# Seven block products of the second feed-forward matrix in digit passes, with some of the low digits made on GpSimd

## The reference, cut to what matters

```python
# first block, for each of its two layers
h = rmsnorm(x, norm_mlp[i])
x = x + jnp.square(jax.nn.relu(h @ w_ff1[i])) @ w_ff2[i]     # 1024 -> 4096 -> 1024
...
# second block, for each of its two layers
def sq_relu_mlp(x, w1, w2):
    return jnp.square(jax.nn.relu(x @ w1)) @ w2
```

## Time and profile before

| | |
|---|---|
| time, median of 3 runs | 1448.4 us (1447.07 to 1448.81) |
| span of the profiled execution, first to last instruction | 1445.8 us |
| TensorE matmul busy | 1414.5 us, 98% of the span |
| VectorE busy | 1092.6 us, 76% |
| ScalarE busy | 815.7 us, 56% |
| GpSimd busy | 289.4 us, 20% |
| mean granted TensorE clock | 0.998 of full |

### The profile page before, as it was taken

The page is one execution under the profiler, slowest core; times in us unless marked ns, Lnnn a source line. Parts: engine busy times, 40 slices in busy tenths (PEclk is TensorE's granted clock), DMA queues, the critical chain, the costliest instruction groups (busy, mean ns, idle before and its releaser), DMA issues.

```text
span 1445.8 us, 20133 instructions
## 1 busy us (share of the span) xinstructions
PE 1414.5 (98%) x8416; PEld 1188.4 (82%) x8416; DVE 1092.6 (76%) x1326; ACT 815.7 (56%) x998; POOL 289.4 (20%) x109
## 2 busy tenths in 40 slices
PE   7999999999999999999999999999999999999997
PEld 5788888888877788888889788688888888888886
DVE  5337667989952365859999769878998857689988
ACT  4565636666445553646657356656666326277662
POOL 4598150000028695410000000000000005000000
PEclk9999999999999999999999999999999999999999
DMA  8833336555546642445756443305565453155551
GB/s 306 302 122 122 139 128 222 204 202 193 189 144 236 214 148 91 156 168 199 234 179 200 167 162 110 137 28 206 204 219 189 151 203 117 46 207 210 207 194 68
DMA packets 121227, 250.28 MB, mean 173 GB/s; under 512 B 15041, under 2 KB 27057, under 8 KB 121009
## 3 DMA queue, kind: packets, MB, share of 16 engines
q1 hardware_dynamic: 120872, 248.90, 48.9%
q10 hardware_dynamic: 264, 0.10, 0.0%
HBM read 247.94 MB, written 1.05 MB: 172 GB/s over the span
## 4 chain that ended last, share of the span: by engine, by line
PE 80%; DVE 11%; ACT 5%; issue 1%; POOL 1%; DMA 1%; DVEq 0%; ACTq 0%
PE psum L522 77%; PE psum L529 4%; DVE w_lo L1283 2%; POOL w_lo L1283 1%; DVE w_lo L1290 1%; DVE w_lo L1393 1%; DVE big L1381 1%; DVE x L1462 1%; ACT w_hi_big L1319 1%; DMA ring<-in_mlp_w 1%; DVE ring L1381 1%; ACT s_hi L1327 1%; DVE big L2962 1%; ACT w_hi_tmp L1253 1%; ACT w_hi_tmp L1263 0%
## 5 line engine op out<-in xcount | busy, mean ns | idle before, releaser
L522 PE MATMUL psum<-ht_hi,w_lo 128*128 128x256 f32 x960 | 279.7, 292 | 5.5 <-ACT work L1337 4.1
L522 PE MATMUL psum<-w_lo,ht_hi 128*128 128x512 f32 (+1 forms) x576 | 222.2, 389 | 0.8 <-DVE w_lo L1283 0.8
L522 PEld LDWEIGHTS psum<-ht_hi,w_lo 128*128 128x128 f32 x960 | 180.0, 187 | 15.5 <-issue 14.4
L522 PEld LDWEIGHTS psum<-w_lo,ht_hi 128*128 128x128 f32 x576 | 108.4, 188 | 22.1 <-DVE w_lo L1283 1.3
L522 PE MATMUL psum<-ht_lo,w_hi_tmp 128*128 128x256 f32 x448 | 125.1, 279 | 0.0
L522 PE MATMUL psum<-ht_lo,w_hi_rows 128*128 128x256 f32 x448 | 125.0, 279 | 0.0
L522 PE MATMUL psum<-ht_hi,w_hi_tmp 128*128 128x256 f32 x448 | 124.8, 279 | 0.0
L522 PE MATMUL psum<-ht_hi,w_hi_rows 128*128 128x256 f32 x448 | 124.8, 279 | 0.0
L1283 POOL TENSOR_TENSOR w_lo<-ring,w_hi_work 128x2048 fp32r<-128x2048 f32 x12 | 57.5, 4789 | 250.3 <-ACT w_hi_work L1263 250.3
L1310 ACT ACTIVATE w_hi_work<-ring 128x2048 fp32r<-128x2048 f32 x28 | 53.6, 1915 | 74.1 <-DMA ring<-in_w_ff 39.1
L522 PEld LDWEIGHTS psum<-ht_lo,w_hi_tmp 128*128 128x128 f32 x448 | 85.2, 190 | 5.8 <-issue 5.7
(11 more groups left out here) (443 smaller groups left out, 3935.4 us busy)
## 6 DMA issues: line engine op xcount, KB each, us to landing
ring<-in_w_ff SPq DMA_DIRECT2D x32, 2048.0 KB, 8.0
ring<-in_mlp_w SPq DMA_DIRECT2D x32, 2048.0 KB, 8.4
ring<-in_w_in SPq DMA_DIRECT2D x19, 2048.0 KB, 7.8
ring<-in_w_out SPq DMA_DIRECT2D x4, 2048.0 KB, 7.7
ring<-in_w_ple_gate SPq DMA_DIRECT2D x4, 2048.0 KB, 7.8
ring<-in_sb_ssm_w_in SPq DMA_DIRECT2D x4, 2048.0 KB, 8.1
ring<-in_dsa_w_in SPq DMA_DIRECT2D x3, 2048.0 KB, 8.0
ring<-in_w_up_nsa SPq DMA_DIRECT2D x2, 2048.0 KB, 8.1
```

Of the source, the lines that this page charges most:

```text
L522: ins = pe.matmul(o, lhsT, rhs, start=start, stop=stop)
```

## The change

- Product seven runs in digits: its two float32 matmuls become six digit passes. For that ScalarE also copies the third weight sum (`t_hi[2]`, last in `act_right_forms`), GpSimd subtracts it (`t_lows[2]`, in the new `pool_mlp_seven`), and VectorE makes the low digits of the second hidden blocks (`dve_hidden_second`, last in the round).
- The low digits of the second half of the columns of ff1.2 to ff1.7 are made by GpSimd in place of VectorE, with a signal of their own (`w_lo_cols`).
- TensorE waits for the two new signals, `second_low` and `last_sum_low`, ahead of bank 6.
- `pool_tail` waits for the first product of the last ff2 tile (`ff2_ready`) in place of the last `form_used`.

```diff
--- before.py
+++ after.py
@@ -147,8 +147,10 @@
 SPLITS = [f"in{c}" for c in range(N_IN)] + ["up_nsa", "up_ret"] + ["out0", "out1"]
 LAST = 7
 SEVEN = ("", "A.", "B.")
-DIGIT_SUMS = 2
-DIGIT_FORMS = 2 + DIGIT_SUMS
+DIGIT_SUMS = 3
+HIGH_FORMS = 2 + DIGIT_SUMS
+LOW_FORMS = HIGH_FORMS - 1
+HIDDEN_FORMS = 4
 
 
 def _seven_tiles(pre):
...
@@ -469,12 +471,15 @@
-    w_lo_ready = sig("w_lo_ready", 2 * (len(SPLITS) - pool_share))
+    column_share = sum(_by_columns(name) for name in SPLITS)
+    w_lo_ready = sig("w_lo_ready", 2 * (len(SPLITS) - pool_share) - column_share)
+    w_lo_cols = sig("w_lo_cols", column_share)
-    t_summed, form_hi, form_lo = sig("t_summed", 4 * LAST), sig("form_hi", DIGIT_FORMS * LAST), sig("form_lo", DIGIT_FORMS * LAST)
+    t_summed, form_hi, form_lo = sig("t_summed", 4 * LAST), sig("form_hi", HIGH_FORMS * LAST), sig("form_lo", LOW_FORMS * LAST)
+    last_sum_low, second_low = sig("last_sum_low", LAST), sig("second_low", LAST)
@@ -607,8 +612,8 @@
                            line.ready if u == 1 and k == KT - 1 else None)
 
         def wait_split(name, half):
-            signal, n = lower_digits(name, splits)
-            pe.wait_ge(signal.sem, st.at(signal, 2 * n + half + 1))
+            signal, n = lower_digits(name, half, splits)
+            pe.wait_ge(signal.sem, st.at(signal, n))
 
         def next_columns(name):
...
@@ -793,22 +798,19 @@
                                  stop and u == 1, signal if u == 1 else None)
 
                 pe.wait_ge(s_low.sem, st.at(s_low, m + 1))
-                pe.wait_ge(form_lo.sem, st.at(form_lo, DIGIT_FORMS * m + 2))
+                pe.wait_ge(form_lo.sem, st.at(form_lo, LOW_FORMS * m + 2))
                 by_digits(bank[5], 2, right_hi[:, :, 1, :], w[:, :, 1, BANK:D], False, None)
                 by_digits(bank[7], 0, right_hi[:, :, 0, :], w[:, :, 0, BANK:D], final, form_used)
-                pe.wait_ge(form_lo.sem, st.at(form_lo, DIGIT_FORMS * m + 3))
+                pe.wait_ge(form_lo.sem, st.at(form_lo, LOW_FORMS * m + 3))
                 by_digits(bank[3], 1, t_hi[0], t_lows[pre][0], final, form_used)
-                if DIGIT_SUMS > 1:
-                    pe.wait_ge(form_lo.sem, st.at(form_lo, DIGIT_FORMS * m + 4))
-                    by_digits(bank[2], 3, t_hi[1], t_lows[pre][1], final, form_used)
-                else:
-                    pe.wait_ge(t_summed.sem, st.at(t_summed, 4 * m + 3))
-                    for u in range(2):
-                        mm(bank[2], s_form(sums_, 3, u), t_sums[pre][1][:, u, :], first and u == 0, final and u == 1,
-                           form_used if u == 1 else None)
-                pe.wait_ge(t_summed.sem, st.at(t_summed, 4 * m + 4))
+                pe.wait_ge(form_lo.sem, st.at(form_lo, LOW_FORMS * m + 4))
+                by_digits(bank[2], 3, t_hi[1], t_lows[pre][1], final, form_used)
+                pe.wait_ge(second_low.sem, st.at(second_low, m + 1))
+                pe.wait_ge(last_sum_low.sem, st.at(last_sum_low, m + 1))
                 for u in range(2):
-                    mm(bank[6], hid_f[:, s + 2 * u + 1, P:S], t_sums[pre][2][:, u, :], first and u == 0, False)
+                    f = s + 2 * u + 1
+                    products(bank[6], hid_hi[:, f, P:S], hid_lo[:, f, P:S], t_hi[2][:, u, :], t_lows[pre][2][:, u, :],
+                             first and u == 0, False, None)
 
             def seven_open(n):
@@ -1263,10 +1265,13 @@
             act.activation(w_hi[place][:, 0:width], ring[n % RING][:, h * width:(h + 1) * width], ACT.Copy) \
                 .then_inc(st.up(w_hi_ready), 1)
 
-    def lower_digits(name, splits):
-
-        mine = [n for n in splits if (n in POOL_SPLITS) == (name in POOL_SPLITS)]
-        return (w_lo_pool if name in POOL_SPLITS else w_lo_ready), mine.index(name)
+    def lower_digits(name, half, splits):
+
+        def signal(n, h):
+            return w_lo_pool if n in POOL_SPLITS else w_lo_cols if h and _by_columns(n) else w_lo_ready
+
+        own = signal(name, half)
+        return own, [(n, h) for n in splits for h in range(2) if signal(n, h) is own].index((name, half)) + 1
 
     def lower_split(st, eng, tiles, splits, name):
@@ -1276,21 +1281,22 @@
     def lower_half(st, eng, tiles, splits, name, h):
 
         n, nth = tiles.index(name), splits.index(name)
-        signal, _ = lower_digits(name, splits)
+        signal, _ = lower_digits(name, h, splits)
         places, width = PLACES if splits is SPLITS else PLACES2, split_halves(name)
         c = slice(h * width, (h + 1) * width)
         eng.wait_ge(w_hi_ready.sem, st.at(w_hi_ready, 2 * nth + h + 1))
         eng.tensor_tensor(w_lo[n % RING][:, c], ring[n % RING][:, c], w_hi[places[name][h]][:, 0:width].bitcast(F32), ALU.subtract) \
             .then_inc(st.up(signal), 1)
 
-    def lower_columns(st, dve, tiles, splits, name, h):
+    def lower_columns(st, eng, tiles, splits, name, h):
 
         n, nth, c = tiles.index(name), splits.index(name), slice(h * S, (h + 1) * S)
-        dve.wait_ge(w_hi_ready.sem, st.at(w_hi_ready, 2 * nth + h + 1))
-        dve.tensor_tensor(w_lo[n % RING][:, :].rearrange("p (k n) -> p k n", k=KT)[:, :, c],
+        signal, _ = lower_digits(name, h, splits)
+        eng.wait_ge(w_hi_ready.sem, st.at(w_hi_ready, 2 * nth + h + 1))
+        eng.tensor_tensor(w_lo[n % RING][:, :].rearrange("p (k n) -> p k n", k=KT)[:, :, c],
                           ring[n % RING][:, :].rearrange("p (k n) -> p k n", k=KT)[:, :, c],
                           w_hi[(PLACES if splits is SPLITS else PLACES2)[name][h]][:, :].rearrange("p (k n) -> p k n", k=KT).bitcast(F32), ALU.subtract) \
-            .then_inc(st.up(w_lo_ready), 1)
+            .then_inc(st.up(signal), 1)
 
     def form_free(st, eng, tiles, pre, n, nth):
@@ -1317,9 +1323,9 @@
         form_free(st, act, tiles, pre, n, 2)
         act.wait_ge(t_summed.sem, st.at(t_summed, 4 * m + 2))
         act.activation(right_hi, blocks(ring[at % RING][:, :])[:, :, :, BANK:D], ACT.Copy).then_inc(st.up(form_hi), 1)
-        if DIGIT_SUMS > 1:
-            act.wait_ge(t_summed.sem, st.at(t_summed, 4 * m + 3))
-            act.activation(t_hi[1], t_sums[pre][1], ACT.Copy).then_inc(st.up(form_hi), 1)
+        for i in (1, 2):
+            act.wait_ge(t_summed.sem, st.at(t_summed, 4 * m + i + 2))
+            act.activation(t_hi[i], t_sums[pre][i], ACT.Copy).then_inc(st.up(form_hi), 1)
 
     def act_hidden_forms(st, act, pre, n):
@@ -1386,10 +1392,10 @@
         at, m = tiles.index(f"{pre}ff2.{n}"), seventh(pre, n)
         w, lo = blocks(ring[at % RING][:, :]), blocks(w_lo[at % RING][:, :])
         forms = [(1, lo[:, :, :, 0:BANK], w[:, :, :, 0:BANK], col_hi), (3, lo[:, :, :, BANK:D], w[:, :, :, BANK:D], right_hi)]
-        forms += [(2 * i + 2, t_lows[pre][i], t_sums[pre][i], t_hi[i]) for i in range(DIGIT_SUMS)]
+        forms += [(2 * i + 2, t_lows[pre][i], t_sums[pre][i], t_hi[i]) for i in range(2)]
         for i in which:
             nth, low, v, hi = forms[i]
-            dve.wait_ge(form_hi.sem, st.at(form_hi, DIGIT_FORMS * m + nth))
+            dve.wait_ge(form_hi.sem, st.at(form_hi, HIGH_FORMS * m + nth))
             dve.tensor_tensor(low, v, hi.bitcast(F32), ALU.subtract).then_inc(st.up(form_lo), 1)
 
     def dve_hidden_sums(st, dve, pre, n):
@@ -1413,6 +1419,12 @@
         dve.wait_ge(hid_hi_ready.sem, st.at(hid_hi_ready, FB // 2 * mlp_nth(pre) + 2 * n + 2))
         dve.tensor_tensor(lo, h, hi.bitcast(F32), ALU.subtract).then_inc(st.up(hid_lo_ready, 2), 2)
 
+    def dve_hidden_second(st, dve, pre, n):
+
+        s = 4 * (n % 2)
+        hi, lo, h = (v[:, s:s + 4, :].rearrange("p (u v) t -> p u v t", v=2)[:, :, 1, P:S] for v in (hid_hi, hid_lo, hid_f))
+        dve.tensor_tensor(lo, h, hi.bitcast(F32), ALU.subtract).then_inc(st.up(second_low), 1)
+
     def dve_hidden_low(st, dve, pre, f):
 
         at = hid_slot(2 * f)
@@ -1433,23 +1445,29 @@
         dve_hidden_sums(st, dve, pre, 0)
         dve_hidden_first(st, dve, pre, 0)
         dve_hidden_sums_low(st, dve, pre, 0)
-        dve_form_lows(st, dve, tiles, pre, 0, range(3, DIGIT_FORMS))
+        dve_form_lows(st, dve, tiles, pre, 0, (3,))
+        dve_hidden_second(st, dve, pre, 0)
         for n in range(1, LAST):
             ahead = f"{pre}ff1.{n + 1}"
             lower_columns(st, dve, tiles, splits, ahead, 0)
-            if n == 1:
-                lower_columns(st, dve, tiles, splits, ahead, 1)
             dve_hidden_sums(st, dve, pre, n)
             dve_hidden_first(st, dve, pre, n)
-            if n > 1:
-                lower_columns(st, dve, tiles, splits, ahead, 1)
             dve_hidden_sums_low(st, dve, pre, n)
             dve_form_sums(st, dve, tiles, pre, n)
-            dve_form_lows(st, dve, tiles, pre, n, range(DIGIT_FORMS))
+            dve_form_lows(st, dve, tiles, pre, n, range(LOW_FORMS))
+            dve_hidden_second(st, dve, pre, n)
         lower_half(st, dve, tiles, splits, f"{pre}ff2.{LAST}", 0)
```

(21 more changed lines are left out.)

## The result

The changed kernel takes **1539.84 us** (median of 4 runs, 1537.46 to 1540.73), the kernel before 1447.89 beside it: a ratio of 1.0619, 95% interval 1.0585 to 1.0654 (1.0635 by these two medians alone). The prediction was 1538, range 1515 to 1562. The profiled span is 1538.1 against 1445.8: 92.3 us longer.

A forecast was written before the change was run, and what follows sets the result against it. VectorE, shut out by GpSimd, was to bound feed-forward rounds. Five rounds of +3.41 (17.05) plus entry 5.35 make 22.4 a part, 89.6 for four; added to 1445.8, plus 2.6, this gives 1538 us, range 1515 to 1562.

The forecast's parts named there:

- The exclusion: Feed-forward rounds: two-SBUF-input VectorE instructions and GpSimd's SBUF-reading ones shut each other out; 6.60 us a round; chance 0.84.
- The price of one instruction: Feed-forward rounds: VectorE loses 4.42 us to GpSimd's moved column half, 2.18 to its third-weight-sum low digits.
- The 2.36 for GpSimd's small instruction: GpSimd's low digits of the third weight sum, 1024 columns: 2.36 us, interpolated between 2.57 at 1120 and 4.61 at 2048.
- The round and the entry: Each feed-forward part: VectorE's round 24.86 against TensorE's 21.45 us, +3.41; start of the second half unit 5.35 later.
- 0 ± 1 a part: End of each feed-forward part: the last product's tail, on either engine, was put at 0 ± 1 us.
- rival 3: Feed-forward rounds: waits over 3 us lower TensorE's clock, up to 34 us on top of the exclusion, 1572; chance 0.06.
- TensorE's 21.45: Feed-forward rounds before the change: TensorE takes 21.45 us a round, read from three rounds totalling 64.35.
- Its threshold: Feed-forward rounds: TensorE stays the bound if GpSimd's instructions cost VectorE less than 3.19 of their 6.97 us a round.
- TensorE's 0.32 a product: Last block product: six digit passes replace two full-precision ones, 1.40 for 1.72 us; −9.0 over 28 products where TensorE bounds.
- Rival 2, ScalarE's copy: Feed-forward rounds: engines run side by side, but the copy delays TensorE 0.95 us in half of 24 rounds; 1455; chance 0.05.
- the "good 3 us" of waiting: Feed-forward rounds, as a sign: TensorE should wait a good 3 us a round for ScalarE's ReLU.
- "and they then take turns.": Where GpSimd and VectorE overlap: one waits for the whole of the other's instruction, whichever came first, then they alternate.

The follow-up runs named there:

- the work on VectorE: The whole change without GpSimd: moved column half and third weight sum's low digits on VectorE, against the changed kernel; 1455.46 us, ratio 1.0046.
- memsets: Changed kernel with each of GpSimd's two subtractions replaced by two memsets of the same destination, reading no SBUF; 1441.35 us, ratio 0.9953.
- those two kernels: Two attention waits added on GpSimd: to the kernel before, 1450.51 us; to the all-on-VectorE kernel with later copy and low digits, 1447.8 us.

## Why the prediction was right

- *The exclusion.* Right, and it is nearly the whole: without GpSimd's reads the loss falls from 92 us to 6.5 (the work on VectorE) or below zero (memsets).
- *The price of one instruction.* 2.18 and 4.42 were predicted; the rows at 293.60 and 303.16 show 4.50 − 2.28 = 2.22 and 4.81 − 0.42 = 4.39. The 2.36 for GpSimd's small instruction was called interpolated, but 1024 columns lie below both sizes that it was worked out from; it fits even so: 3.13 less 0.78 of waiting, until VectorE's next starts at 293.60, is 2.35.
- *The round and the entry.* 24.86 predicted, 24.59 to 24.77 measured; 5.35 predicted, and 5.42 measured at the first entry, 5.4 at two others and 4.7 at that of the third part. Entries and rounds together make 87.6 where 89.6 were predicted. The other 4.7 of the 92.3 lie outside them, where the sum had 0 ± 1 a part: 3.4 behind TensorE's last wait in the last three parts (see rival 3), and 1.3 between the parts. So two small errors of opposite sign bring the total closer than its terms, and that much is luck. TensorE's 21.45 is that of the first part; the other three take 21.34.
- *Its threshold.* The sum has the cost begin where VectorE's round passes TensorE's. The same sum gave 1477 and 1473 for GpSimd's two instructions alone, and 1477 and 1472 were measured, though their losses add up to little over half of that of both.
- *TensorE's 0.32 a product.* −9.0 by the rows, −7 measured alone. Rightly not counted in the change.
- *Rival 2, ScalarE's copy.* Its mechanism exists, with the cause that the prediction read from the earlier trace rows, and its size was about right: 0.95 in half of the 24 rounds is 11, and alone the copy cost 14 in entries and rounds. In the changed kernel it counts at the entry only, since VectorE sets the rounds.
- *Rival 3, the clock.* It falls, as the rows at 318 to 326 show; the mean granted clock over the span is 0.979 against 0.998. In the rounds this is hidden: the "good 3 us" of waiting that the prediction expected in each are 3.3 to 3.45 in some and 1.4 to 1.6 in those behind a fall, the difference being used by the slower passes. It shows where no later wait hides it: after the last waits of the last three parts (3.3 to 3.45) the granted clock is 0.65 to 0.71 over some four microseconds, and the part ends 1.1 later; after that of the first part (1.58) it stays at 1.00 and nothing is lost. Not every long wait is followed by a fall: after one of 3.45 at 806.70 it stays at 1.00.
- *"and they then take turns."* Right in the rounds, where GpSimd's instructions come one at a time; wrong in general, as the 12.23 show. Had GpSimd had a row of instructions there, the sum could have been too small.

## What to carry to other kernels

An idle engine is not free capacity: look first for places where it and its neighbour work at the same time, and compare durations there with those where the neighbour works alone. A cost that two engines share begins only when the slower one passes the bound of the stage, so costs measured one at a time need not add up; add the work and compare it with the bound. And a copy on a third engine is free only if what it waits for, and what stands behind it, both have slack.

## What the runs showed of the hardware that was not expected

An instruction of VectorE that waits for GpSimd isn't let in at GpSimd's next instruction boundary in every execution: 0.69 became 12.23, over ten instructions of GpSimd in a row. In the same place of both layers of the other nine profiled kernels without the waits it took 2.05 to 2.14, so it got in at the first boundary. Two waits on GpSimd that order the engines there remove the split of 15 us in a kernel's times (none of 24 executions in the upper group). That the upper executions of every kernel come from this stage is seen in one trace and otherwise inferred from those two kernels. What decides who gets in was not found.
